# Two transformer blocks in one kernel: norms by halves of the tokens behind a split last output, one joint root between the blocks, and a gelu that advances one tile per step

## The reference, cut to what matters

```python
def _rmsnorm(x, g, eps=NORM_EPS):
    y = x * lax.rsqrt(jnp.mean(x * x, axis=-1, keepdims=True) + eps)
    return y * g

def first_block(x, ...):
    h = _rmsnorm(x, norm_mix)
    ...                                             # three mixers, merged
    x = x + merged @ w_o
    x = x + _conv_ffn(_rmsnorm(x, norm_ffn), ...)   # norm "ffn"
    return _rmsnorm(x, norm_final)                  # norm "fin"

def second_block(x, c, ...):
    h = x
    for l in range(2):
        mod = (jax.nn.silu(c) @ ada_w[l] + ada_b[l]).reshape(B, 3, 3, 1, D)
        n = _modulate(_rmsnorm_2(h, norm_g[l, 0]), mod[:, 0, 0], mod[:, 0, 1])      # s00, s10
        h = h + 0.5 * mod[:, 0, 2] * _swiglu(n, ffn_w_in[l, 0], ffn_w_out[l, 0])
        n = _modulate(_rmsnorm_2(h, norm_g[l, 1]), mod[:, 1, 0], mod[:, 1, 1])      # m0, m1
        z = n @ mix_w_in[l]
        ...                                         # y_a = attention, y_b = gated MLP
        h = h + mod[:, 1, 2] * (merged @ w_out[l])
        n = _modulate(_rmsnorm_2(h, norm_g[l, 2]), mod[:, 2, 0], mod[:, 2, 1])      # s01, s11
        h = h + 0.5 * mod[:, 2, 2] * _swiglu(n, ffn_w_in[l, 1], ffn_w_out[l, 1])
    return _rmsnorm_2(h, final_g)                                                    # out

def _gmlp(uv, ln_g, ln_b, ws, bs):
    u, v = jnp.split(jax.nn.gelu(uv), 2, axis=-1)
    v = _layernorm(v, ln_g, ln_b)
    w = ws * jnp.tril(jnp.ones((128, 128)))
    ...
```

## Time and profile before

| what | value |
|---|---|
| median of three runs | 3565.91 us (3563.82 to 3568.29) |
| profiled execution, its own time | 3562.11 us |
| its span from first to last instruction | 3560.3 us |
| PE busy | 3367.5 us, 95% |
| DVE busy | 1796.7 us, 50% |
| ACT busy | 1283.1 us, 36% |
| mean granted TensorE clock | 0.977 |
| DMA | mean 102 GB/s |

### The profile page before, as it was taken

The page is one execution under the profiler, slowest core; times in us unless marked ns, Lnnn a source line. Parts: engine busy times, 40 slices in busy tenths (PEclk is TensorE's granted clock), DMA queues, the critical chain, the costliest instruction groups (busy, mean ns, idle before and its releaser), DMA issues.

```text
span 3560.3 us, 45484 instructions
## 1 busy us (share of the span) xinstructions
PE 3367.5 (95%) x19392; PEld 2675.9 (75%) x19392; DVE 1796.7 (50%) x2920; ACT 1283.1 (36%) x2081; POOL 105.1 (3%) x202
## 2 busy tenths in 40 slices
PE   6898979999999899999899999999999989999998
PEld 4767745887888688877567788878888756778887
DVE  4545765567757565644754533343333465453333
ACT  4231365434535422223543322233222344332222
POOL 0000000010000011100000000000000000000000
PEclk9999989999999999999999999999999999999999
DMA  3010111454443265633112222222322311223222
GB/s 135 26 50 13 49 41 58 160 201 160 143 164 136 93 247 195 236 117 116 46 48 77 83 101 95 96 82 101 97 98 95 114 51 48 72 83 100 96 95 71
DMA packets 100538, 363.99 MB, mean 102 GB/s; under 512 B 11632, under 2 KB 11696, under 8 KB 99696
## 3 DMA queue, kind: packets, MB, share of 16 engines
q1 hardware_dynamic: 75888, 272.14, 22.5%
q0 software_dynamic: 24448, 88.95, 7.5%
HBM read 358.94 MB, written 2.10 MB: 101 GB/s over the span
## 4 chain that ended last, share of the span: by engine, by line
PE 88%; DVE 8%; ACT 3%; issue 1%; DMA 0%; DVEq 0%; POOL 0%; ACTq 0%; POOLq 0%
PE ps_run L414 86%; PE ps_run L695 1%; DVE nrm L1734 1%; DVE HL L1734 1%; ACT nrm L1060 1%; DVE wl L1727 1%; ACT wh L1060 0%; DVE ug L1727 0%; DVE AL L1727 0%; DVE dP L2055 0%; DVE nst L2345 0%; ACT ug L1060 0%; ACT nP L1060 0%; DVE cp L1727 0%; DVE HL L1727 0%
## 5 line engine op out<-in xcount | busy, mean ns | idle before, releaser
L414 PE MATMUL ps_run<-HH,wh 128*128 128x512 f32 x2608 | 1052.1, 403 | 48.7 <-DVE HL L1734 28.9
L414 PE MATMUL ps_run<-HH,wl 128*128 128x512 f32 x2608 | 1026.3, 394 | 0.0
L414 PE MATMUL ps_run<-HL,wh 128*128 128x512 f32 x2608 | 1026.2, 393 | 0.0
L1727 DVE TENSOR_TENSOR wl<-st,wh 128x1024 fp32r<-128x1024 f32 x511 | 625.3, 1225 | 769.4 <-ACT wh L1060 769.1
L1060 ACT ACTIVATE wh<-st 128x1024 fp32r<-128x1024 f32 x511 | 538.0, 1054 | 723.9 <-PE ps_run L414 718.8
L414 PEld LDWEIGHTS ps_run<-HH,wh 128*128 128x128 f32 x2608 | 496.0, 190 | 180.8 <-DVE HL L1734 51.2
L414 PEld LDWEIGHTS ps_run<-HH,wl 128*128 128x128 f32 x2608 | 496.1, 190 | 106.7
L414 PEld LDWEIGHTS ps_run<-HL,wh 128*128 128x128 f32 x2608 | 497.3, 191 | 103.6 <-issue 6.7
L414 PE MATMUL ps_run<-AH,wh 128*128 128x512 f32 x1104 | 431.0, 390 | 0.0
L414 PE MATMUL ps_run<-AH,wl 128*128 128x512 f32 x1104 | 429.7, 389 | 0.0
L414 PE MATMUL ps_run<-AL,wh 128*128 128x512 f32 x1104 | 429.5, 389 | 0.0
(11 more groups left out here) (405 smaller groups left out, 3286.0 us busy)
## 6 DMA issues: line engine op xcount, KB each, us to landing
st<-wst SPq DMA_DIRECT2D x511, 512.0 KB, 3.3
mb<-ada POOLq DMA_DIRECT2D x144, 512.0 KB, 4.6
cw<-cw POOLq DMA_DIRECT2D x4, 1024.0 KB, 6.2
X<-xT SPq DMA_DIRECT2D x8, 256.0 KB, 7.6
X<-xT POOLq DMA_DIRECT2D x8, 256.0 KB, 5.7
out<-X SPq DMA_DIRECT2D x8, 256.0 KB, 2.1
kc<-kc POOLq DMA_DIRECT2D x1, 1139.0 KB, 6.4
mb<-cond POOLq DMA_DIRECT2D x2, 512.0 KB, 5.1
```

The source lines that it names most:

```text
L414: i = self.e.matmul(out, lhsT, rhs, start=start, stop=stop, skip_group_check=True)
L1727: self.e.tensor_tensor(out, a, b, op).then_inc(*self.w.done(*points))
```

## The change

Seven things change, and the work that is computed stays the same.

1. The last output before a norm is made in two passes over its blocks, first for tokens 0 to 255, then for 256 to 511 (`last_linear`). Between the passes PE sums the squares of the left half (`squares_left`); the sum of the right half comes later (`squares_right`).
2. X[7], its square, the root, the scaling and both splits of the norm are made by halves (`square_half`, `root_half`, `scaled_halves`, `high_halves`): sixteen pieces of 256 tokens in place of eight of 512.
3. The first two outputs behind a norm are made together, left half of both, then right half of both (`two_linear`).
4. Between the blocks X is no longer normalised before s00: while the feed-forward ends, a second set of squares is made, weighted by the square of the first norm's gain plus 1e-6, so that one root over them (with 1e-12) serves both norms. X itself is rewritten later (`final_norm` is now a filler of DVE in the next feed-forward). The silu of the second layer's condition (`modulation(1)` on ACT) moves behind the norm s00.
5. In the mixer the permuted product of a rope stands two products behind its own, not one.
6. The gelu of v's tiles takes five steps of one tile each, two steps later, and PE's part of gated begins five steps later.
7. The mask of `tril` is made by DVE inside the layer norm, before the four products sv and not right ahead of them.

```diff
+    def two_linear(self, keys, specs, hi, lo, norm, ring):
+        outs = [self.bank(key, ring) for key in keys]
+        n = len(specs[0])
+        blocks = [[self.weights(s[i]) for s in specs] for i in range(n)]
+        for h in range(2):
+            tt = part(h)
+            for i in range(n):
+                self.w.wait_ge("lo", norm, n * h + i)
+                end = h and i == n - 1
+                for key, out, (wh, wl, used) in zip(keys, outs, blocks[i]):
+                    self.mm(out[:, tt], wh, hi[i][:, tt], i == 0, False)
+                    self.mm(out[:, tt], wh, lo[i][:, tt], False, False)
+                    self.mm(out[:, tt], wl, hi[i][:, tt], False, i == n - 1, *([key] if end else []), *(used if h else []))
+                if h == 0 and i == 1:
+                    self.squares_right(sums_for(norm))
+
+    def last_linear(self, key, specs, hi, lo, ready, ring, after):
...
+        for h in range(2):
+            tt = part(h)
+            for i, (wh, wl, used) in enumerate(blocks):
...
+            if h == 0:
+                self.squares_left(after)
...
-    def squares_summed(self, key):
...
+    def squares_left(self, key):
...
+        for k, out, t in self.parts:
+            w.wait_ge("six squares", k)
+            self.mm(out, ones, t[2], True, False)
+        for k, out, t in self.parts:
+            w.wait_ge("sq", k, 6)
+            self.mm(out, ones, t[0], False, False)
+        self.squares_of_last(0)
...
     def mixer(self, l):
...
-            while ropes:
-                self.rope((key, ropes.pop()), "perm64", m.nrm[0], 512, (4, 5))
+            self.rope((key, ropes.pop(0)), "perm64", m.nrm[0], 512, (4, 5))
...
     def gated(self, l):
...
-        yield
+        for _ in range(6):
+            yield
...
+    def high_halves(self, key, shift=None):
...
+        for n in range(16):
+            if n == 3:
+                self.square_half(group, 1)
+            if n == 5:
+                self.root_half(group, 1)
+            w.wait_ge("scaled", key, n)
...
     def down(self, after, half):
         if half:
             self.table()
         for i in range(8):
+            if half and i == 7:
+                self.square_half(after, 0)
+                self.root_half(after, 0)
             finish(self.spend(11))
-            if half:
+            if half and i < 7:
...
+    def scaled_halves(self, key, gain, shift=None):
...
+        for n in range(17):
+            if n == 1:
+                self.late_split()
+            if n == 3:
+                self.late_half()
+            if n < 16:
+                if n % 8 == 0:
+                    w.wait_ge("inverse std", key, n // 8)
...
+                self.stt(tmp[n % len(tmp)], x[n], gain(n % 8), rs[n // 8], MUL, MUL, ("scaled", key, n))
+            if n:
...
+    def last_output(self, key, after, into, split):
+
+        def take(h):
+            self.w.wait_ge(*key, h)
+            into(7, self.ps(*key)[:, part(h)], part(h), *([("free", key)] if h else []), ("x", after, 7, h))
+
+        take(0)
+        self.late_half = lambda: take(1)
+        self.late_split = split
...
-        for tb in range(4):
-            self.gelu_inner(m.ugate_v[tb], (key, "gv", tb), (key, "v gelu a", tb), (key, "v gelu b", tb))
-        yield
-        for tb in range(4):
-            self.gelu_outer(m.ugate_v[tb], (key, "gv", tb), (key, "v gelu c", tb))
-        yield
+        yield
+        yield
+        for tb in range(5):
+            if tb < 4:
+                self.gelu_inner(m.ugate_v[tb], (key, "gv", tb), (key, "v gelu a", tb), (key, "v gelu b", tb))
+            if tb:
+                self.gelu_outer(m.ugate_v[tb - 1], (key, "gv", tb - 1), (key, "v gelu c", tb - 1))
+            yield
```

More of the change, by code:

```diff
@@ L387, in drawn, with part, halves, sums_for @@
         next(side, None)
+def part(h):
+    return slice(256 * h, 256 * h + 256)
+def halves(tiles):
+    return [t[:, part(h)] for h in range(2) for t in tiles]
+def sums_for(key):
+    return "fin" if key == "s00" else key
 def pairs_of(x):
@@ L839, in ffn @@
         dense = (0, 1, 2, 3, 4)
-        ready = [("lo", key, i) for i in range(8)]
         for half in range(2):
@@ L859, in mixer @@
         nm = ("mix_w_in_2", (l,))
-        ready = [("lo", f"m{l}", i) for i in range(8)]
         dense = (0, 1, 2, 3)
@@ L1011, in program @@
         self.ffn("ffn", "fin", ("ffn_w_up", (0,)), ("ffn_w_down", (0,)))
-        for i in range(8):
-            self.sums("s00", i, 8, m.nrm)
         self.ffn("s00", "m0", ("ffn_w_in_2", (0, 0)), ("ffn_w_out_2", (0, 0)))
@@ L1490, in down, with square_weighted @@
         for i in range(8):
+            if half and i == 7:
+                self.square_half(after, 0)
+                self.root_half(after, 0)
             finish(self.spend(11))
-            if half:
+            if half and i < 7:
                 self.w.wait_ge("x", after, i)
                 self.square_kept(after, i)
+                if after == "fin":
+                    self.square_weighted(i)
         self.cur.pad()
-    def final_norm(self):
+    def square_weighted(self, i):
         m, w = self.m, self.w
-        self.root("fin", m.nrm[2])
-        self.table()
-        for i in range(8):
-            w.wait_ge("x", "s00", i)
-            self.square("s00", i, m.X[i], m.nrm)
+        w.wait_ge("final scales")
+        if i >= 2:
+            w.wait_ge("sq taken", "s00", i - 2)
+        w.own()
+        self.act(m.nrm[3 + i % 2], m.nrm[i % 2], ACT.Copy, ("sq", "s00", i), scale=m.nf2[:, i:i + 1])
     def shift(self, l, sub):
@@ L1509, in swiglu @@
         m, w = self.m, self.w
-        self.root(key, m.nrm[2])
-        w.wait_ge("pe ffn", key, 0)
-        self.high(key, 8, m.nrm[3:6], m.HH, self.shift(l, sub))
+        self.high_halves(key, self.shift(l, sub))
+        if key == "s00":
+            self.modulation(1)
         for half in range(2):
@@ L1712, in program @@
         self.swiglu("s11", "out", 1, 2)
[L1713 removed]
+        self.square_half("out", 1)
+        self.root_half("out", 1)
 class Dve:
@@ L2235, in conv_ffn @@
                 self.rest(("ffn", "f", g), m.cv[par], m.AH[j], m.AL[j])
-            self.down("ffn", "fin", half, lambda i, b, *points: self.tt(m.X[i], b, m.X[i], ADD, *points), fill)
+            self.down("ffn", "fin", half, self.added_into, fill)
     def down(self, key, after, half, into, fill):
         for i in range(8):
+            if half and i == 7:
+                next(fill, None)
+                self.last_output((key, "down", half, i), after, into, lambda: self.end_split())
+                return
             finish(self.spend(11))
@@ L2512, in program @@
         self.swiglu("s11", "out", 1, 2, iter(()))
-        self.root("out")
-        for i in range(8):
-            self.stt(m.X[i], m.X[i], m.V("final_g", i), m.nrm[2], MUL, MUL, ("y", i))
+        for h in range(2):
+            w.wait_ge("inverse std", "out", h)
+            for i in range(8):
+                x = m.X[i][:, part(h)]
+                self.stt(x, x, m.V("final_g", i), m.nrm[2][:, part(h)], MUL, MUL, *([("y", i)] if h else []))
+                if h == 0 and i == 6:
+                    self.late_half()
 class Pool:
```

196 lines of the change are left out of this document (137 added, 59 removed).

## The result

The median of the changed kernel is 3518.47 us (3517.45 to 3521.55, four runs), that of the kernel before in the same comparison 3567.03 (3563.82 to 3568.29). The ratio is 0.9867, 95% interval 0.985 to 0.9884: 48.6 us faster. A later comparison of the same kernel (e5) gave 0.9867 again. The profiled execution took 3521.55 us, its span is 3519.8; against the 3560.3 of before that is 40.5. Why the medians lie further apart than the profiles is answered at the end.

The account below looks back on a forecast made before the run. The prediction took PE's waits at the seams, a latency chain over 512 tokens and then DVE's pace, as the loss. Its terms summed to 42.2 us, taking the profiled 3562.1 to 3520, named 3523 for the runs' higher median; range 3507 to 3544.

Parts of the forecast that it names:

- ffn: Seam ahead of the feed-forward, its pieces subtractions without a shift: from 26.4 us to 21.1, a gain of 5.3.
- s00: Seam between the blocks, where a second norm's sums followed the first: from 46.0 us to 31.5, a gain of 14.5.
- m0, s10, m1: Three seams behind `down`: each from 29.3 us to 25.1, a gain of 4.2 each, 12.6 in all.
- s01, s11: Two seams behind `back`, slab made ahead: each from 27.2 us to 22.3, a gain of 4.9 each, 9.8 in all.
- products ahead of v, v: Mixer products with the rope one product later: wait covered except at v, a loss of 1.6 us twice, -3.2.
- weave, gelu, mask: Attention woven with the gated MLP: 2 us gained per mixer, 4 in all, bounds -4 and +6 each.
- out: End of the kernel: stores already run at the DMA limit, ending 7.2 us behind the first, a loss of 0.8 us.
- rival 3: 256-column matmuls are bound by weight loads, costing 81 us more at 0.188 each, time 3593 us; chance 0.02.
- rival 2: At the seams, DVE's and ACT's pieces wait 0.15 us more each: 17 us less gain, 3540 us; chance 0.08.
- now 21.1: Step at the feed-forward's seam: the stretch that took 26.4 us before would take 21.1 after the change.
- Rival 1: Seams win as said but the weave loses 4 us per mixer: 12 us less gain, 3535 us; chance 0.10.

Follow-up runs that it names:

- e5: The changed kernel itself run once more, nothing changed: 3519.51 us, ratio 0.9867.
- e3: The changed kernel with the last output ahead of each norm made in one pass of 512 columns, the norm still by halves: 3549.84 us, ratio 0.9962.
- e6: The changed kernel with four places changed (second condition's silu, DVE's filler ahead of the last output, DVE's last rope, stores by halves): 3509.93 us, ratio 0.9839.
- e2: The kernel before with only the joint root between the blocks and the second condition's silu moved behind the norm, all on 512 tokens: 3555.16 us, ratio 0.9977.
- e9: The kernel of e1 run once more, nothing changed: 3528.57 us, ratio 0.9899.
- e1: The changed kernel with the gelu of v's tiles, PE's filler and the mask woven as before: 3532.29 us, ratio 0.9915.
- e10: e6 with the slab that the third product waits for rounded earlier and subtracted by POOL in place of DVE, at four seams: 3519.33 us, ratio 0.9872.

## Why the prediction was right

The measured column lays the two profiles side by side by the start of each third product, which in before is the first output's end plus 24 x 0.227, and for the weave by W1 and W2. Gains in us, forecast and measured:

| term | forecast | profiles |
|---|---|---|
| ffn | 5.3 | 3.6 |
| s00 | 14.5 | 15.8 |
| m0, s10, m1 | 12.6 | 4.35 + 4.33 + 4.29 = 13.0 |
| s01, s11 | 9.8 | 5.0 + 4.35 = 9.35 |
| products ahead of v, v | -3.2 | -3.6 |
| weave, gelu, mask | 4 | 3.2 + 1.9 = 5.1 |
| out | -0.8 | -1.2 |
| sum | 42.2 | 42.1 |

The start of the program took 1.6 us longer in the profile of after, which leaves the 40.5. That the sums agree to the tenth is luck: ffn and s00 are off by -1.7 and +1.3.

- **The seams.** Right in mechanism and in size: first tile, pieces 0.79 apart for 0.81, one wait of 0.64 to 0.73 ahead of the third product for about 1. The passes over the last output gave 0.120 us for a matmul of 256 columns (24 in 3138.34 - 3135.47 = 2.87 us at s11), next to the 0.117 that was chosen and far from 0.154, where rival 3 would have decided. That PE waits less than 1 us ahead of its first tile and keeps its clock came true, and e3 shows what it is worth: of 4.3 us at s10 about 1 goes with the clock. At s11 the gain is 4.35 for 4.9 because PE waits there for something that the prediction did not have, the PSUM bank of the last output, which DVE gives back when it has taken X[7]'s right half:

```profile
3144.74 0.39 PE L435 MATMUL ps_run<-HH,wh 128*128 128x256 f32 x1 [0.92 <-DVE X L1857]
```

The estimate of rival 2, 0.15 a piece, did not show.
- **ffn.** The term was mis-sized at its step "now 21.1", which measured 22.8. It took X[7]'s half 0.2 us behind the left pass, as at s10; DVE had a slab and a filler ahead of it, and took it 1.95 behind. e6 gave back 1.15 of it by moving one line.
- **s00.** The gain is almost all that of e2 (14.3): the second series of sums, which the prediction named, and the silu and table loads ahead of the first root, some 3.7 us, which its reading of the 33.09 us left out. Halves add only 1.5 there, for the silu now stands ahead of the third product's slab: 3.03 us of wait for the 3.4 forecast, and 0.67 in e6.
- **v and out.** The waits were there as worked out, 1.39 for 1.6 and 7.3 us behind the first store for 7.2; e6 shows that both were a matter of order.
- **The weave.** Right in sign and mis-sized: 4 forecast, 5.1 in the one pair of profiles, 6.7 by PE's idle time and 10.3 on average over twelve profiles, the last with the low clock of e2 and e9 in it. Rival 1 (a loss of 4 each) is out. The medians lie 48.6 apart and the profiles 40.5, because the profiled execution of before (3562.11) lay 4.9 us under the median of its kernel's runs, and that of after (3521.55) 3.1 above. With 10.3 in place of 5.1 the table comes to 47.3, so the clock in the weave may be what sets the profiled pair apart from the medians; no trace of the other executions shows it.
- **The change itself.** Four table loads fewer on ACT (46 to 42) and 16 sum records between the blocks for 22, as forecast.

## What to carry to other kernels

Where one engine must wait for a chain of latencies and then for another engine's pace, cut both: hide the chain under a second pass over the last output, and give the waiting engine two outputs per piece; either cut alone brought 0.1 to 0.6 us of 4.4 behind `down` here. After it, read each seam for what still stands ahead of the first or behind the last piece on the pacing engines (a filler, a silu and a rope were worth 5.5 us here, by moving single lines). Where the clock can differ between executions of one kernel, compare stretches and the idle time within them, not whole times.

## What the runs showed of the hardware

- The same code ran the stretch 540 to 550 at a clock of 0.50 in one execution (e1) and 1.00 in another (e9), and the first came 8.7 us later to the first seam.
- The same attention code, with the same 19.5 us of idle time on PE, took 336 us at a mean clock of 0.97 (before) and 343 at 0.95 (e2).
- PE's clock did not fall at waits of 0.48 to 0.92 us ahead of the first tile (1.00 in each stretch of after at the seams); after one of 4.10 us (e3) the stretch 2380 to 2385 ran at 0.54. Waits between these went both ways: after one of 2.04 us (e10, s10) the stretch had 0.66, after one of 2.06 (e10, s01) 1.00. After the 3.03 us at s00 it stayed at 1.00 in after and was 0.74 from 1230 to 1235 in e9, with the same instructions there.
- A DVE instruction over 256 elements stretched from 0.48 to 2.27 us beside one of POOL that took 2.35. The Trainium skill, "SBUF — State Buffer", section SBUF: two separate sides, has the two engines share a pair of ports, for a DVE instruction with two inputs in SBUF, of which the first to start keeps the other out for its whole instruction; the rows agree, for POOL began 0.36 us earlier and DVE ended 0.28 us behind it.
